# Partition sums of a modulation vector: thirty-two one-column products, or eight 512-column products with a masked fold

## The reference

```
c_act = silu(c)                       # 2048
mod   = c_act @ w_ada + b_ada         # 2048 x 12288, in both blocks
sh1, sc1, g1, sh2, sc2, g2 = split(mod, 6)
h = rms_norm(x, g) * (1 + sc1) + sh1
...                                   # projections, S5 branch, attention, merge
x = x + g1 * (merged @ w_out)
h2 = rms_norm(x, norm_mlp_g) * (1 + sc2) + sh2
x = x + g2 * (square(relu(h2 @ w_ff1)) @ w_ff2)
x = rms_norm(x, norm_final_g)
...                                   # second block: mod of its own, mixer, mixture of 16384 experts
```

## Time and profile before

| | |
|---|---|
| runs | 3493.39, 3495.85 and 3503.64 us; median 3495.85 |
| profiled execution | span 3494.1 us from its first to its last instruction |
| PE busy | 2382.4 us (68%) |
| PEld busy | 2035.6 us (58%) |
| DVE busy | 2875.2 us (82%) |
| ACT busy | 1009.5 us (29%) |
| POOL busy | 1259.2 us (36%) |
| mean granted TensorE clock | 0.818 |

### The profile page before, as it was taken

One profiled execution on the slowest core, in us unless ns is written; L12 is line 12 of the kernel. 1 busy time (PEld: TensorE's weight loads), 2 busy tenths in 40 slices (PEclk: granted clock), 3 DMA queues, 4 the chain that ended last, 5 costly groups with the idle time before them and its releaser, 6 DMA issues.

```text
span 3494.1 us, 38094 instructions
## 1 busy us (share of the span) xinstructions
PE 2382.4 (68%) x14750; PEld 2035.6 (58%) x14750; DVE 2875.2 (82%) x3467; ACT 1009.5 (29%) x1529; POOL 1259.2 (36%) x975
## 2 busy tenths in 40 slices
PE   8869999989899999999989899300044430003444
PEld 7859999988788888888989779200011110001111
DVE  7698867867886886887777857899999999998777
ACT  1404433434644544453565545100000000000000
POOL 6351101101110110110000000468866788887663
PEclk7779999989999999999999999655567665556777
DMA  9517968868796996896454245899999999999998
GB/s 362 211 25 284 343 241 297 328 242 286 263 324 242 325 326 240 316 324 210 157 170 133 83 159 188 326 383 427 427 427 427 407 427 425 427 427 427 427 427 346
DMA packets 223692, 1069.00 MB, mean 306 GB/s; under 512 B 24344, under 2 KB 30488, under 8 KB 157592
## 3 DMA queue, kind: packets, MB, share of 16 engines
q0 software_dynamic: 119808, 704.70, 50.6%
q1 hardware_dynamic: 103704, 361.87, 29.0%
HBM read 1062.80 MB, written 3.67 MB: 305 GB/s over the span
## 4 chain that ended last, share of the span: by engine, by line
PE 52%; DVE 18%; POOL 15%; DMA 9%; issue 4%; ACT 2%; DVEq 0%; SPq 0%; ACTq 0%
PE ps L593 52%; POOL wide L1734 6%; DMA wide<-in_up,idx_t 5%; DVE acts L2611 5%; POOL wide_b L1734 4%; POOL raws L1734 3%; DMA wide_b<-in_up,idx_t 2%; DVE wide L2539 1%; POOL a_acc L1734 1%; DMA a_raws<-in_ada 1%; DVE a_raws L2468 1%; DVE a_acc L1774 1%; DMA raws<-in_up,idx_t 1%; DVE a_raws L2465 1%; ACT acts L1274 1%
## 5 line engine op out<-in xcount | busy, mean ns | idle before, releaser
L593 PE MATMUL ps<-opa_both,w_hi 128*128 128x256 f32 (+1 forms) x5024 | 1153.8, 318 | 44.1 <-DVE opa_both L1833 23.9
L1750 DVE TENSOR_TENSOR raws_r<-raws,w_hi 128x1024 fp32r<-128x1024 f32 x607 | 729.2, 1224 | 286.0 <-ACT w_hi L1213 281.8
L593 PEld LDWEIGHTS ps<-opa_both,w_hi 128*128 128x128 f32 x5024 | 832.4, 194 | 107.2 <-issue 41.3
L593 PE MATMUL ps<-opa_both,raws_r 128*128 128x256 f32 x3152 | 883.4, 284 | 0.0
L1213 ACT ACTIVATE w_hi<-raws 128x1024 fp32r<-128x1024 f32 x607 | 637.8, 1057 | 710.8 <-PE ps L593 440.8
L593 PEld LDWEIGHTS ps<-opa_both,raws_r 128*128 128x128 f32 x3152 | 609.5, 193 | 7.4
L1649 POOL DMA_DIRECT2D a_raws<-in_ada x320 | 169.2, 529 | 1183.3 <-DVE a_acc L1774 925.8
L593 PE MATMUL ps<-opb_both,w_hi 128*128 128x512 f32 (+1 forms) x1952 | 578.3, 361 | 4.8 <-DVE opb_both L2434 4.8
L593 PE MATMUL ps<-opb_both,raws_r 128*128 128x256 f32 x1616 | 442.3, 282 | 0.0
L1774 DVE SCALAR_TENSOR_TENSOR a_acc<-a_raws,csil,a_acc 128x1024 f32<-128x1024 f32 x317 | 400.9, 1297 | 15.1 <-DMA a_raws<-in_ada 15.0
L593 PEld LDWEIGHTS ps<-opb_both,w_hi 128*128 128x128 f32 x1952 | 343.4, 190 | 57.2 <-DVE opb_both L2434 5.7
(11 more groups left out here) (438 smaller groups left out, 3411.1 us busy)
## 6 DMA issues: line engine op xcount, KB each, us to landing
raws<-in_w SPq DMA_DIRECT2D x607, 512.0 KB, 4.6
a_raws<-in_ada POOLq DMA_DIRECT2D x320, 512.0 KB, 5.8
a_raws<-in_ada SPq DMA_DIRECT2D x28, 512.0 KB, 8.5
raws<-in_ada SPq DMA_DIRECT2D x24, 512.0 KB, 9.5
acts<-in_ada SPq DMA_DIRECT2D x12, 512.0 KB, 7.8
x_res<-in_xT SPq DMA_DIRECT2D x1, 2048.0 KB, 12.6
out<-x_res SPq DMA_DIRECT2D x2, 1024.0 KB, 24.2
wide<-in_up,idx_t POOLq DMA_INDIRECT x109, 25.9
```

The source lines that it names most:

```text
L593: return nc.tensor.matmul(out, lhs, rhs, start=start, stop=stop)
L1750: TT(w_lo[p % RAW].rearrange("p b n -> p (b n)"), raw[p % RAW], w_hi[p % HI][:, :, :].rearrange("p b n -> p (b n)").bitcast(F32), ALU.subt ...
```

## The change

`ones[:, 0:32]` becomes the stationary operand and `a_acc` the moving one. Each product has 512 columns of `a_acc` and writes 32 equal rows of PSUM, at partitions 32j to 32j+31 for column tile j; two banks of four tiles hold the 4096 sums. DVE then masks these two banks with a constant that keeps column i of each 32 in the partitions that are i modulo 32 (`fold`), reduces over i to 32 values a partition (`fold_r`), and spreads these over a fourfold wider array with zeros (`fold_e`, by the constant `quarter`). Four products of 32 x 32 with `fold` as the stationary operand bring the outputs to the layout that `ada_cols` expects. The first strip of `a_acc` serves as scratch for the masked values.

The schedule of the steps moves too: steps run from beat 5 to beat 47 instead of 2 to 44, `ada_cols` goes from beat 1 to beat 5, and group 2's steps are done in merge rounds 4 to 15, 16/3 a round.

```
 def beat_ada(b):
-    b -= 2
+    b -= 5
     return (min(64, 3 * max(b, 0) // 2), min(64, 3 * max(b + 1, 0) // 2))
...
                     if beat is not None and (beat + j) % BEATS == 0:
-                        ada_sums(2 + (beat + j) // BEATS)
+                        ada_sums(2 + (beat + j) // BEATS, (4, 7))
+                    if beat is not None and (beat + j) % BEATS == 5:
+                        ada_fold(2 + (beat + j) // BEATS)
...
-            def ada_sums(g):
+            def ada_sums(g, banks):
                 pe.wait_ge(S["ada"], 64 * (g + 1) - len(ON_PE))
                 pe.wait_ge(S["adacol"], g)
-                for h in range(HALVES):
-                    for b in range(8):
-                        m = mm(ps[:, 7, 8 * h + b:8 * h + b + 1], a_acc[:, h, b * P:(b + 1) * P], ones[:, 0:1],
-                               True, True)
+                for r in range(2):
+                    for j in range(4):
+                        at = (j % 2) * 512
+                        m = mm(ps[32 * j:32 * j + 32, banks[r], :], ones[:, 0:32],
+                               a_acc[:, 2 * r + j // 2, at:at + 512], True, True)
+                m.then_inc(S["adarow"], 1)
+
+            def ada_fold(g):
+                pe.wait_ge(S["adafold"], g)
+                for i in range(4):
+                    m = mm(ps[32 * i:32 * i + 32, 7, 0:32], cst("fold"),
+                           fold_e[:, :, :, :, i].rearrange("p r j c -> p (r j c)"), True, True)
                 m.then_inc(S["adaps"], 1)
...
                 if n == 3:
-                    ada_sums(1)
+                    ada_sums(1, (6, 7))
                 for g in range(2):
                     merge_gate(n, g)
                 if n == 3:
+                    ada_fold(1)
                     pe.wait_ge(S["adacol"], 2)
...
-            ada_sums(5)
-            linear(PAN["xr"], GRP["in2"], opa, 8, ready=("op", 28, 2), swapped=True)
+            ada_sums(5, (4, 7))
+            linear(PAN["xr"], GRP["in2"], opa, 8, ready=("op", 28, 2), swapped=True,
+                   between=lambda j: ada_fold(5) if j == 3 else None)
...
+            def ada_rows(g, b0):
+                dve.wait_ge(S["adarow"], g)
+                wide_e = a_acc[:, 0, :].rearrange("p (r a i) -> p r a i", r=2, i=32)
+                link(TT(wide_e, ps[:, b0:8:7 - b0, :].rearrange("p r (a i) -> p r a i", i=32),
+                        cst("fold").unsqueeze(1).unsqueeze(1).broadcast_to([P, 2, 16, 32]), ALU.mult))
+                link(V.tensor_reduce(fold_r[:, :, :, :].rearrange("p r c s -> p r (c s)"), wide_e, AX.X, ALU.add))
+                for r in range(2):
+                    ins = TT(fold_e[:, r], fold_r[:, r].unsqueeze(1).broadcast_to([P, 4, 4, 4]),
+                             cst("quarter").unsqueeze(2).unsqueeze(2).broadcast_to([P, 4, 4, 4]), ALU.mult)
+                    ...
             def on_beat(b):
                 if at == 1:
+                    ada_rows(g - 1, 4)
+                if at == 5:
                     ada_cols(g - 1)
...
-                q0, q1 = (120 + 4 * n, 124 + 4 * n) if n < 2 else (128 + 5 * max(n - 3, 0), min(128 + 5 * max(n - 2, 0), 192))
+                q0, q1 = (120 + 4 * n, 124 + 4 * n) if n < 2 else (128 + 16 * max(n - 4, 0) // 3, 128 + 16 * max(n - 3, 0) // 3)
                 rest_to(base + 2 + AHEAD)
                 if n == 3:
-                    ada_cols(1)
+                    ada_rows(1, 6)
                 ada_steps(q0, (q0 + q1) // 2)
                 rest_to(base + 4 + AHEAD)
+                if n == 3:
+                    ada_cols(1)
...
             operand(2, root3)
-            ada_cols(5)
+            ada_rows(5, 4)
...
             conv(0)
+            ada_cols(5)
```

More of the change, by code:

```diff
@@ L285 @@
 CON_N = (("ident", P), ("swap", P), ("rope_cos", T), ("rope_sin", T), ("causal", 3 * P), ("cmp_add", 2 * 16),
-         ("cmp_mul", 2 * 16), ("bucket", 384), ("iota16", 16))
+         ("cmp_mul", 2 * 16), ("bucket", 384), ("iota16", 16), ("fold", 32), ("quarter", 4))
 def _consts():
@@ L302 @@
 small xload rload bload land0 land1 land2 land3 land4 land5 aland0 aland1 aland2 aland3 aland4 aland5 bland0 bland1 bland2 bland3 hi lo panel freed_a freed_d init sigc csl ada adan
-adaps adacol sq ss mean rs nt nh op chain_v chain_p chain_a par ang sin bf ab k0 k0c bt btc cs cx vmm wdone prod
+adaps adarow adafold adacol sq ss mean rs nt nh op chain_v chain_p chain_a par ang sin bf ab k0 k0c bt btc cs cx vmm wdone prod
 ymm yadd yg ghi glo gmul msig mterm hid fhalf fsum ffc line_ps line line_out bias vt vtc sc sm ex pn tp ptc pv ov
@@ L354, in constants @@
     put("bucket", hot)
+    put("fold", np.tile(np.eye(32, dtype=np.float32), (4, 1)))
+    put("quarter", np.repeat(np.eye(4, dtype=np.float32), 32, 0))
     put("iota16", np.broadcast_to(np.arange(16, dtype=np.float32), (P, 16)))
@@ L385, in build @@
         cs = sb("cs", [P, 3, 16])
+        fold_r = sb("fold_r", [P, 2, 4, 4])
+        fold_e = sb("fold_e", [P, 2, 4, 4, 4])
         with ExitStack() as over:
@@ L1775, in ada_steps @@
                     ins.then_inc(S["ada"], 1)
+            def ada_rows(g, b0):
[7 more added lines that the diff above has]
+                             cst("quarter").unsqueeze(2).unsqueeze(2).broadcast_to([P, 4, 4, 4]), ALU.mult)
+                    if r == 0:
+                        link(ins)
+                    else:
+                        ins.then_inc(S["adafold"], 1)
             def on_beat(b):
```

## The result

| | median | runs | ratio to before, 95% interval |
|---|---|---|---|
| before | 3499.65 us | 3490.36 to 3507.81, 20 runs | |
| after | 3486.04 us | 3480.55 to 3501.58, 20 runs | 0.9968 [0.9959, 0.9976] |

The change wins 0.3% (13.6 us between the medians); 30.4 us or 0.9% were forecast, and 3486 lies outside the range of 3458 to 3484. The profiled execution of the changed kernel has a span of 3484.8 us, 9.3 less than before.

The account below looks back on a forecast made before the run. PE's stream of panels was taken as the bound. Groups 1 to 4 win 9.5, 8.4, 7.0 and 8.6 us, group 5 loses 3.1: 30.4 us off 3495.85, about 3465.5 us; range 3458 to 3484.

Parts of the forecast that it names:

- Sums: On PE, sixteen tiled records taking 2.2 us plus two tiling switches of 0.2 us: 2.6 us a group.
- Rival 1: At the new sums, column tiles do not overlap: 4.7 us more a group, 3484 us; chance 0.12.
- Fold: On PE, four small products behind each sum: 0.1 us, with two tiling switches 0.5 us.
- trip to DVE in round 3: Group 1: PE waits for `adacol` right behind the fold, one trip to DVE and back, 0.7 us.
- Clock: Panels behind the sums of groups 1 to 4 no longer run at low clock: 7.5 us won.
- rival 2: PE's clock still falls in or behind the tiled products, so the 7.5 us stay: 3475 us; chance 0.10.
- Group 2: Last merge round: two more steps on DVE ahead of the out stage, 1.7 us paid, bounds 0 and 2.6.
- Group 5: `ada_rows(5)` on DVE directly ahead of the first `xr` remainder: 2.6 us paid; with the fold's 0.5, cost 3.1.
- DVE's row work in groups 2 to 4: `ada_rows` at beat 1, 2.8 us a group on DVE, hidden because no steps stand there: 0.
- the steps' shift by three beats: Steps end at beat 47 instead of 44; the next sum has 3.2 us to spare, so 0.
- rivals 3 and 4: 3: DVE's added work is not hidden, 3475 us, chance 0.08; 4: sums wait for last steps, about 3501, chance 0.03.

Follow-up runs that it names:

- e5: The changed kernel with 224 unused bytes a partition behind `fold_e`, putting every large buffer at remainder 0 modulo 256; 3466.49 us, ratio 0.9916.
- e7: e5 with the added steps of group 2 spread over merge rounds 3 to 15 and `ada_rows(5)` 12 chunks later; 3463.66 us, ratio 0.9905.
- e16: e5 with `wide` and `w_hi` alone moved to remainder 32 modulo 256; 3458.20 us, ratio 0.9894.
- e18: e7 with 56 unused floats between `a_acc` and `wide` instead of behind `fold_e`, and 8 floats ahead of `wide_b`; 3445.85 us, ratio 0.9859.
- e11: The kernel before, one-column products of groups 2 to 4 issued in four parts over four beats, with the later steps; 3485.83 us, ratio 0.9956.
- e14: e5 with `idx_t` alone moved to remainder 32 modulo 256; 3474.47 us, ratio 0.9937.

## Why the prediction was wrong

The direction and the stream were right, the size was not. The step that failed is in the prediction's first paragraph, that an instruction between two panels delays all that follows, the gathers of the last third too, and so that what the stream wins arrives at the end. The sum took the 30.4 us off the span, and so assumed that the last third takes as long as before. The change declares two buffers and lengthens `con`; I listed what its instructions cost and gave its bytes no term. They moved the destinations of the gathers to remainder 32, and the gathers ran at 420 GB/s instead of 427: 18.0 of the 19.4 us that are lost behind the first cast. With the bytes filled up to remainder 0 (e5) the same instructions give 3466.5 us. Neither the range nor any rival had a case in which an untouched stage changes its rate.

Point by point, by the terms of the sum:

- Sums: 2.6 us forecast, 1.85 measured. The factor is 3.5 instead of 3.2, and a switch of tiling costs less than the 0.2 us taken from the earlier trace rows, at most 0.1: a fold of 0.23 us has two of them in it. Rival 1 is excluded.
- Fold: 0.5 forecast, 0.23 measured; trip to DVE in round 3: 0.7 forecast, a wait of 0.31 measured.
- Clock: won in groups 1 to 4 as forecast; rival 2 did not occur. But the clock fell in `xr`, for which the sum has no term. PE restarts there at 0.50 behind the 3.99 us and does 20 records in 4 us; until about 1648.5 that loses some 2.5 us. In the kernel before the wait at this place is 1.43 us and the clock behind it 1.00 (1675 to 1677 us), so PE does not restart low wherever it has waited, as rival 2 has it. Here the longer wait cost its own time and the clock behind it.
- Group 2: 1.7 us forecast, 3.9 measured between these two traces (13.19 against 9.32). DVE idled for data there as well, 1.67 us ahead of 741.48 and 0.85 ahead of 743.62, both for `a_raws`, which the forecast did not have; over all kernels the term is some 2 us (section on e7).
- Group 5: 2.6 us forecast, 2.56 measured (3.99 against 1.43), without the clock.
- DVE's row work in groups 2 to 4, and the steps' shift by three beats: hidden, 0, as forecast; rivals 3 and 4 did not occur. Rows of DVE at group 5, where its length is seen (1.22 + 1.22 + 0.48 = 2.9 us, forecast 2.8):

```profile
1638.38 1.22 DVE L1798 TENSOR_TENSOR a_acc<-ps,con 128x1024 f32<-128x1024 f32 x1
1639.63 1.22 DVE L1800 TENSOR_REDUCE fold_r<-a_acc 128x32 f32<-128x1024 f32 x1
1640.89 0.48 DVE L1802 TENSOR_TENSOR fold_e<-fold_r,con 128x64 f32<-128x64 f32 x2
```

The better terms (0.75 and 0.27 a group in four groups, 0.4 in round 3: 4.5 us) and the worse (2.2 and 2.5) nearly cancel; they would give 30.2 us, and 28.7 came by the first cast, 27.3 by the second. That e5 lands 1 us from the forecast therefore confirms the sum of the stream, not each term, and some of that closeness is luck.

## What to carry to other kernels

A new buffer or a longer table is an edit to every buffer declared behind it. Before pricing its instructions, compare the addresses before and after, and where a stage runs at a DMA share of 1.0, check that its destinations still start on 256-byte boundaries; then compare the time of each stage, since the end alone showed a small gain where 28.7 us were won and 19.4 lost. Choose the mark between two stages with care: a mark inside the last projection still missed up to 5 us of a falling clock. Reductions by one-column products are better streamed: ones as the stationary operand on four column tiles took 1.85 us instead of 9 to 11 and kept the clock. Where they must stay, short parts between the panels kept the clock as well (e11).

## What the hardware showed that I had not expected

- Gathered rows of 8192 bytes that start 32 bytes behind a 256-byte boundary: 420 GB/s instead of 427, and by the packets of e16 and e18 only from the fourth gather in a row on.
- The start address of `raws_r` against those of `w_hi` and the operand, 32 bytes apart within a block or not: 578 or 568 records in 100 us of a full PE at clock 1.00, worth 0.5% (some 17 us) in the kernel before.
- e5 and e14 have the same instructions. In one the clock is 1.00 from 2172 to 2180 us, in the other 0.50, which costs 5.4 us; whether the addresses or chance decide is not shown.
- Column tiles of 32 with 512 fp32 columns each: 3.5 times the whole array (1.85 us for 6.46), also when two products in a row use the same tile (1.88).
